# Linear attention, its closing product and the feed-forward written as one block, with the first closing tile between the last attention chunks

## The reference

```python
def second_block(x, ...):                    # one layer here
    x = x + gla_mixer(rms_norm(x, norm_mix), *mix_params)
    x = x + sqrelu_mlp(rms_norm(x, norm_ffn), w1, w2)
    return rms_norm(x, final_norm)

def gla_mixer(h, w_in, w_gk_up, b_gk, g_onorm, w_out):
    q, k, v, r, gk_low = split(h @ w_in)     # 4 heads: 128 columns of q, k; 256 of v, r
    log_a = log_sigmoid(gk_low @ w_gk_up + b_gk) / 16
    ...                                      # per chunk: o = attn(q, k, decay) @ v + q_dec @ state; state carried on
    o = rms_norm(o, g_onorm).reshape(B, S, GLA_DV)
    return (o * jax.nn.silu(r)) @ w_out      # 1024 x 1024

def sqrelu_mlp(h, w1, w2):                   # 1024 -> 4096 -> 1024
    return jnp.square(jax.nn.relu(h @ w1)) @ w2
```

## Time and profile before

| what | value |
|---|---|
| runs (3) | 2702.56 us median, 2702.14 to 2705.46 |
| profiled execution | 2696.63 us, of which the span is 2694.8 us |
| PE busy | 2591.0 us of the span, mean granted clock 0.983 |
| DVE, ACT, POOL busy | 1145.4, 863.6, 424.1 us |
| attention of the second block: last `project_vr` issued until | 1836.77 us from the span's start |
| closing product | first matmul at 1870.79 us |
| feed-forward | first matmul 1985.91, last 2686.77 us |

### The profile page before, as it was taken

How to read it: one execution, slowest core, us unless ns; L and a number is a source line. 1 busy time by engine, 2 the same in 40 slices (tenths; PEclk the granted TensorE clock), 3 DMA queues, 4 the chain that set the end, 5 groups by cost and what they waited for, 6 DMA issues and landing times. The chain is left out here.

```text
span 2694.8 us, 36214 instructions
## 1 busy us (share of the span) xinstructions
PE 2591.0 (96%) x13200; PEld 2194.9 (81%) x13200; DVE 1145.4 (43%) x2217; ACT 863.6 (32%) x1567; POOL 424.1 (16%) x891
## 2 busy tenths in 40 slices
PE   8999999999999999999798999997989999999998
PEld 7888888888878987888675888886768888888887
DVE  4333333323323411777544767654333333333334
ACT  5322222223213424555333444432231221112212
POOL 4444444443001305000010001101000000000000
PEclk9999999999999999999898999998989999999999
DMA  6211111111523121222152110102431111111111
GB/s 233 72 49 53 54 49 60 49 59 59 193 96 106 60 90 37 61 66 60 57 166 87 51 57 26 47 26 92 164 133 47 63 39 46 47 54 54 39 47 70
DMA packets 73682, 196.82 MB, mean 73 GB/s; under 512 B 8112, under 2 KB 29808, under 8 KB 72816
## 3 DMA queue, kind: packets, MB, share of 16 engines
q1 hardware_dynamic: 73584, 195.50, 22.1%
HBM read 153.53 MB, written 37.75 MB: 71 GB/s over the span
## 5 line engine op out<-in xcount | busy, mean ns | idle before, releaser
L1064 PE MATMUL ra_qkv_ps<-ra_wh,ra_xl 128*128 (+1 forms) x512 | 206.7, 404 | 11.6 <-DVE ra_wl L899 9.2
L2891 PE MATMUL ff_f_ps<-x_upper,ff_w1l 128*128 128x512 f32 x512 | 200.5, 392 | 6.2 <-DVE ff_w1l L2827 6.2
L1064 PE MATMUL ra_qkv_ps<-ra_wh,ra_xh 128*128 (+1 forms) x512 | 201.1, 393 | 0.0
L1064 PE MATMUL ra_qkv_ps<-ra_wl,ra_xh 128*128 (+1 forms) x512 | 200.4, 391 | 0.0
L2891 PE MATMUL ff_f_ps<-x_lower,ff_w1h 128*128 128x512 f32 x512 | 200.1, 391 | 0.0
L2891 PE MATMUL ff_f_ps<-x_upper,ff_w1h 128*128 128x512 f32 x512 | 200.1, 391 | 0.0
L2904 PE MATMUL ff_y_ps<-ff_w2h,ff_hl 128*128 128x512 f32 x512 | 199.2, 389 | 0.0
L2904 PE MATMUL ff_y_ps<-ff_w2l,ff_hh 128*128 128x512 f32 x512 | 199.2, 389 | 0.0
L2904 PE MATMUL ff_y_ps<-ff_w2h,ff_hh 128*128 128x512 f32 x512 | 199.2, 389 | 0.0
L2854 DVE TENSOR_TENSOR ff_acc<-ff_y_ps,ff_acc 128x1024 f32<-128x1024 f32 x64 | 78.4, 1225 | 213.9 <-PE ff_y_ps L2904 213.9
L2795 ACT ACTIVATE ff_relu<-ff_f_ps 128x512 f32<-128x512 f32 x64 | 38.3, 598 | 378.0 <-PE ff_f_ps L2891 378.0
(11 more groups left out here) (400 smaller groups left out, 6579.0 us busy)
## 6 DMA issues: line engine op xcount, KB each, us to landing
staging<-in_w_ff SPq DMA_DIRECT2D x64, 512.0 KB, 3.9
ra_raw<-in_w_in_a SPq DMA_DIRECT2D x30, 768.0 KB, 4.6
gated_a<-ra_sg SPq DMA_DIRECT2D x64, 128.0 KB, 1.9
staging<-in_w_vr_c SPq DMA_DIRECT2D x16, 512.0 KB, 4.0
wa_gin<-gated_a SPq DMA_DIRECT2D x6, 1024.0 KB, 4.9
staging<-in_w_out_a SPq DMA_DIRECT2D x9, 512.0 KB, 4.6
staging<-in_x_cols SPq DMA_DIRECT2D x8, 512.0 KB, 5.5
ra_opening<-in_x SPq DMA_DIRECT2D x8, 512.0 KB, 7.7
```

Source lines behind the costliest of these rows:

```text
L1064: last = pe.matmul(out, a[:, kt, t * P:(t + 1) * P], b[:, ds(slot, 1), kt, at:at + n].rearrange("p a n -> p (a n)"), start=(kt == 0 and i ...
L2891: last = pe.matmul(f_ps[j % 2][:, :], a[:, kt, f * P:(f + 1) * P], b[:, kt, half * HALF:(half + 1) * HALF], start=(kt == 0 and i == 0), st ...
```

## The change

The three functions become one block in which each engine runs the attention's program, then the closing one's, then the feed-forward's, without a meeting between them. `gla_heads` and `feed_forward` return one program for each engine, and a new function `gla_closing` stands between them; the function `close_mixer` is untouched and still serves the first block.

- All tiles have fixed places in SBUF, so that later tiles lie over earlier ones as these come free; the waits on the other function's semaphores (`gl.…`, `wc.…`) say when. The PSUM banks are shared likewise; the feed-forward's `inner` banks are the ones that held the transposed gated tiles (`wc_g_ps`).
- `meanwhile(engine, t)` is called in the last head, and in the steps that follow it: PE transposes gated tile 0 at t = 5 and tile 1 at t = 7, and multiplies tile 0 in three pieces (weight rows 0 to 2, 3 to 5, 6 and 7) ahead of the last three `attend`. ACT and DVE split the eight rows of `w_out` at t = 0, 1, 2, 5, 7, 7, 8, 9.
- The last head's gated tiles are no longer written to memory: PE transposes them from `gl_sr`. `gated_c` holds three heads.
- Tiles 1 to 7 are written out, without a loop; `transpose_x` of a tile comes after weight rows 4 and 6 of the next one (before: 2 and 5 of the one after).
- `later(engine, t)` splits the first four feed-forward weight pieces in rounds 2, 3 and 7 of the closing. The first `inner` starts right after closing tile 7, and tile 7's own `transpose_x` comes behind it.
- `ff_acc` is eight tiles with a load each. The last feed-forward chunk is taken out of PE's loop, and in its last row tile the two halves of 512 columns come one after the other: each is added, squared and scaled apart, and stored apart.

```diff
-        gla_heads(nc, xT, gain("g_mix"), ...)
-        close_mixer(nc, "wc_", gated_c, t["w_out_c"], gain("g_onorm"), x2, None, ident, neghalf, staging,
-                    arrived["close_c"], loads("ffn", [pieces(t["w_ff1"], i, 2) for i in range(2)]), x3, xT=xT)
-        feed_forward(nc, x3, xT, ...)
+        @block.tensor
+        def _(pe):
+            heads[4](pe, wc.meanwhile[3])
+            wc.programs[4](pe)
+            last[4](pe)
...
+        for s in range(LAST, LAST + 3):
+            meanwhile(pe, s - LAST + NT)
+            attend(s - 3, s % NT + NT - 3, 1)
+            if s < LAST + 2:
+                scores(s - 2, H - 1, s % NT + NT - 2, 1)
...
+    def tensor_meanwhile(pe, t):
+        if t in (5, 7):
+            for half in range(2):
+                transpose_g(pe, (t - 5) // 2, half)
+        if t >= 8:
+            for kt in ((0, 1, 2), (3, 4, 5), (6, 7))[t - 8]:
+                multiply(pe, 0, kt)
+
+    def tensor(pe):
+        for t in range(1, NT):
+            for kt in range(KW):
+                multiply(pe, t, kt)
+                if kt in (4, 6):
+                    transpose_x(pe, t - 1, kt // 6)
+                if kt % 4 == 3 and t + 1 < NT:
+                    transpose_g(pe, t + 1, kt // 4)
...
+    def vector_meanwhile(dve, t):
+        if t < 3:
+            w_lower(dve, t)
+        if t == 5:
+            w_lower(dve, 3)
+        if t == 6:
+            for half in range(2):
+                g_lower(dve, 0, half)
+        if t == 7:
+            w_lower(dve, 4)
+            for half in range(2):
+                g_lower(dve, 1, half)
+            w_lower(dve, 5)
+        if t in (8, 9):
+            w_lower(dve, t - 2)
...
+    def load_row(sp, kt):
+        if kt >= 2:
+            sp.wait_ge(wl_done, kt - 1)
+        else:
+            sp.wait_ge(gl.wl_done, gl.pieces)
+        sp.dma_start(staging[:, kt % 2, :], w[kt * P:(kt + 1) * P, :]).then_inc(raw_in[kt % 2], 16)
+
+    def load_res(sp, t):
+        if t < 2:
+            sp.wait_ge(gl.attend_mm, GLA_HEADS * NT)
+        else:
+            sp.wait_ge(y_done, t - 1)
+        sp.dma_start(xin[:, t % 2, :], x[t * P:(t + 1) * P, :]).then_inc(res_in[t % 2], 16)
...
+    def vector(dve, later):
+        for t in range(1, NT):
+            finish(dve, t - 1)
+            scale_x(dve, t - 1)
+            if t + 1 < NT:
+                g_lower(dve, t + 1, 0)
+            later(dve, t)
+            for half in range(2):
+                x_lower(dve, t - 1, half)
+            if t + 1 < NT:
+                g_lower(dve, t + 1, 1)
+        finish(dve, NT - 1)
+        scale_x(dve, NT - 1)
...
+        for j in range(8):
+            inner(0, j, True)
+            if j == 0:
+                wc.split[2](pe)
```

More of the change, by code:

```diff
@@ L2835, in square_of, with vector_later, vector, groups @@
+    def vector_later(dve, t):
+        if t in (2, 3):
+            w_lower(dve, 0, t - 2)
+        if t == NT - 1:
+            w_lower(dve, 0, 2)
+            w_lower(dve, 0, 3)
+    def vector(dve):
+        def groups(c, first):
+            for j in range(8):
                 dve.wait_ge(relu_done, 8 * c + j + 1)
@@ L2837, in square_of @@
                                          ALU.mult).then_inc(sq_done, 1)
-            def h_lower(c, j):
+                if first and j == 0:
+                    for half in range(2):
+                        wc.split[1](dve, NT - 1, half)
                 dve.wait_ge(hh_done, 8 * c + j + 1)
@@ new lines, in vector @@
+        groups(0, True)
+        dve.wait_ge(x_in, 16 * NT)
+        with dve.Fori(1, NC) as c:
+            for t in range(NT):
+                add(c - 1, t)
+                if t < 4:
+                    w_lower(dve, c, t)
+            groups(c, False)
+        dve.wait_ge(final_in, 16)
+        for t in range(NT - 1):
+            add(END, t)
+            if t:
+                scale_out(t - 1)
+        halves = [slice(half * HALF, (half + 1) * HALF) for half in range(2)]
+        for half, at in enumerate(halves):
+            dve.wait_ge(y_mm, NT * END + NT + half)
+            dve.tensor_tensor(acc[NT - 1][:, at], y_ps[(NT - 1) % 2][:, half, :], acc[NT - 1][:, at],
+                              ALU.add).then_inc(y_added, 1)
+            if half == 0:
+                scale_out(NT - 2)
@@ new lines, in build, with _ @@
+        wc = gla_closing(place, sems, (g_ps, y_ps, x_ps), xT, t["w_out_c"], gain("g_onorm"), x2, ident, neghalf, staging,
+                         arrived["close_c"], x3, gated_c, gl)
+        later, last = feed_forward(place, sems, (g_ps, y_ps), x3, xT, gain("g_ffn"), t["w_ff1"], t["w_ff2"], t["g_final"],
+                                   neghalf, staging, arrived["ffn"], out, gl, wc)
+        block = whole.enter_context(nc.Block())
+        @block.sync
+        def _(sp):
+            heads[0](sp, wc.meanwhile[0])
+            wc.programs[0](sp, later[0])
+            last[0](sp)
@@ new lines, in _ @@
+        @block.scalar
+        def _(act):
+            heads[1](act, wc.meanwhile[1])
+            wc.programs[1](act, later[1])
+            last[1](act)
+        @block.gpsimd
+        def _(pool):
+            heads[2](pool)
+            wc.programs[2](pool)
+            last[2](pool)
+        @block.vector
+        def _(dve):
+            heads[3](dve, wc.meanwhile[2])
+            wc.programs[3](dve, later[2])
+            last[3](dve)
+        @block.tensor
[3 more added lines that the diff above has]
+            last[4](pe)
```

1437 lines of the change are left out of this document (830 added, 607 removed).

## The result

The changed kernel takes 2656.77 us (median of 4, 2654.57 to 2661.45), the kernel before 2703.35 us (median of 4 on the same chip, 2702.14 to 2705.46): ratio 0.9829, 95% interval 0.9812 to 0.9846, so 46.6 us or 1.7% less. The forecast was 2664.6 us, 2659 to 2673. 3.7 of them come from how I carried one execution over to the median, 2.6 from the terms of the sum (2.2 from one of them), and 1.5 are an earlier start of the stretch that the sum was about.

What follows compares the result with a forecast made beforehand. TensorE was taken as the bound, losing 41.6 us of 850.0 to waits and lower clock. 41.6 - 2.1 - 2.5 + 1.0 = 38.0 us saved, taken off the median: 2664.6 us, range 2659 to 2673.

Steps and rivals of the forecast that it cites:

- What bounds the kernel, and the work of the part: TensorE bounds; from last `project_vr` to last matmul, 850.0 us hold 808.4 of work, 41.6 lost to waits and lower clock.
- Pieces between the chunks: Closing tile 0's pieces of 4.08, 4.08 and 2.72 us each cover a gathering of 2.02 us before the last `attend`s.
- Weight row 7: New PE wait of about 2.1 us in closing tile 0, because DVE splits this row only behind the last gathering.
- First residual: New PE wait of 2.5 us in closing tile 1: the load follows the last `attend` and takes 5.3 us.
- Cover of the rounds: In closing rounds 2 to 7 the scaled tile is ready 1.2 to 1.6 us before PE wants it, so hidden.
- The seam to the feed-forward: The first feed-forward matmul comes within 0.3 us of the closing's last; the former 4.6 us split wait goes.
- The end: Halving the last row tile's add, square, scaling and store saves 1.0 us after the last matmul.
- From the span to the median: The 5.9 us by which the earlier median exceeded its profiled execution also applies to the changed kernel.
- clock falls at the two waits: Rival, chance 0.18: PE's clock drops at the two new waits, 2.4 us a fall, giving 2667 to 2670 us.
- Rounds not covered: Rival, chance 0.11: ACT and DVE lack 1 us in each of seven closing rounds, 7 us; 2668 to 2676 us.
- Pieces not hidden: Rival, chance 0.05: late weight rows make tile 0's pieces wait, 6.6 us return and clock is lost; about 2676 us.
- Slower through a clock that isn't granted: Rival, chance 0.02: TensorE without pauses isn't granted full clock; at 0.94 the time would be 2716 us.

Runs made afterwards that it cites:

- whole_end: The changed kernel with its last row tile multiplied, added, squared, scaled and stored in one instead of halves: 2655.92 us, ratio 0.9843 to the kernel before.
- pad_4: The changed kernel with four unneeded ACT squares of 512 columns added ahead of the square of each of tiles 0 to 6: 2665.94 us, ratio 0.9867.
- bare_chunks: The changed kernel with closing tile 0 multiplied in one go after the last `attend`, not in three pieces between the last chunks: 2665.63 us, ratio 0.9862.
- before_look_1: The kernel before, no edit, one further profiled execution: span 2704.8 us, with 855.11 us from the first `attend` after the last `project_vr` to the last matmul.

## Why the prediction missed, point by point

**What bounds the kernel, and the work of the part** (808.4 us): right, and near by luck. With the one order mended the part is 808.51 us. But the 14.7 us for transposes counted tile 0's two groups, 0.9 us, which the prediction itself puts ahead of the part; without them its sum is 807.5, and the work took 1.0 us more.

**Pieces between the chunks**: right. No wait for `gl_aT`; undone, they cost 7.3 us by the trace, or 9.6 without the 2.3 us for row 7 and the residual that are not lost there; 6.5 of them are waits, the rest goes with the clock of 0.89.

**Weight row 7** (2.1 us): right, 1.97, and it is only the order of two splits.

**First residual** (2.5 us): this term was mis-sized. It is 0.3. I took the median landing of the earlier trace rows, 5.3 us, for a transfer that is issued when SP has issued nothing for over 15 us; 3.25 was the case, near the 3.7 of the weight rows that I had as the lower bound. The step that failed is taking a median over transfers issued under load for one that isn't. The Trainium skill (DMA: Bandwidth & Descriptors, Latency and other measured facts) says that a lighter load on the memory makes the fixed cost of a transfer smaller; 3.25 us on an idle queue and 4.4 with one transfer in flight ahead go that way, but don't tell the fixed cost from the time that the bytes take.

**Cover of the rounds** (1.2 to 1.6 us): held, and is 1.7 to 1.8.

**The seam to the feed-forward**: right. 0.23 us from the closing's last matmul to the first of the feed-forward, and 10.5 us when the splits stand behind it.

**The end** (1.0 us): 1.3.

**The sum** was 38.0 and the same terms measured are 39.3 + 1.3 = 40.6 us against the same execution of before. The span went down by 42.0, since the part also starts 1.5 us sooner. Counted by what was changed, it reads otherwise: the heads begin 2.3 us sooner in code left alone, the last head has 0.8 us more to do, and the change itself gives 42.0 - 2.3 = 39.7 us.

**From the span to the median**: this step failed. I added to the changed kernel the 5.9 us by which the medians of before stood over its profiled execution, as if they went with the chip or the run. By the five profiled executions, 2.4 of them are the part (mean 852.4 for 850.0, the mildest of the five), which the change takes away, and 2.2 are its start (mean 1838.96 for 1836.77), which it leaves; the remaining 1.3 are the three timed runs, which lay above the later mean. The new block has nothing of the first kind: its part is 810.75 to 810.82 us in three profiled executions (whole_end's among them), and its first median is 2.2 us above its profiled execution. Against the mean of the five the part gives 852.4 - 810.8 = 41.6 and the end 1.3, less the 0.9 that were moved ahead of it: 42.0 us. The 59 timed executions of before in the four jobs have a mean of 2701.1, the nine of after, from the first timing and one of the jobs, 2656.7: 44.4 us. The 2.4 us between have no shown cause; by the profiled executions they lie ahead of the part, where the kernels with the last chunk outside the loop start their heads 2.0 us sooner in the mean. The first medians' 46.6 are another 2.2 more, and chance in so few executions is enough for that. The interval, 41.6 to 50.8 us, takes in all of these.

**The range** (2659 to 2673) was worked out from the bounds of two terms and the 3.3 us spread of three runs. Over 59 executions before spreads from 2694.8 to 2706.4. A range against the median of three has to hold that.

**The rivals**: clock falls at the two waits (0.18): no. Rounds not covered: no. Pieces not hidden: no. Slower through a clock that isn't granted: no, 1.00 throughout.

## What to carry to other kernels

A seam where PE waits costs its waits and a clock that may or may not come back between them, so it also makes the time uncertain: filling it is worth more in the median than one mild trace shows. Before carrying an offset between a profiled execution and a median over to a changed kernel, ask which stretches make it, and whether the change removes them; two or three more profiled executions of the kernel before tell. And before calling a part's work counted right, count both kernels between the same instructions: what the change moves across the cut looks like a gain. A transfer's price is that of the transfers which meet the same load, not a median over all.

## What the hardware showed that I had not expected

- Waits of the same length did and didn't cost clock. Two waits of 2.0 and 2.59 us, with 10 us of mostly full-width matmuls between, left it at 1.00 (pad_4); in bare_chunks waits of 1.34 and 2.90 us left the instructions behind them at 0.70 us and one of 2.21 doubled them nearly, 1.22; before_look_1 has the same waits as the first profile of before and PE was busy 2.9 us longer there, at a clock of 0.69 for 0.86.
- The 376 us of the four heads, where PE is busy over 99% of the time, took 3.6 us longer in one execution than in another at a clock of 0.98 for 0.99. In before_look_1 the clock is 0.83 from 1470 to 1490 us and 0.89 from 1720 to 1735, where PE is busy 19.32 of 20.00 and 15.00 of 15.00 us; in the execution of the prediction it is 1.00 in both. What lets it fall there isn't visible in the trace.
- One transfer of 512 KB landed within 3.25 us of its issue when SP had issued nothing for over 15 us, and within 4.4 us when one other, issued 3.0 us ahead, was in flight.
